# Two transformer blocks in one kernel: products of the weight tiles in chunks of six between the attention steps

## The reference

```python
h = rmsnorm(x, norm_mix[i])
mkv = mem_n @ w_mem_kv[i]                    # 256 memory tokens, 4 heads of 64
proj = h @ w_in[i]                           # q, k, v, qm
y_tok = windowed_gqa(q, k, v, sink)          # i = 0: 12 heads, 4 of k and v, ALiBi, a sink logit
y_tok = neighbourhood_attn(q, k, v, rpb)     # i = 1: 12 heads, a table of biases and a window
y_mem = memory_attn(qm, mk, mv)              # 4 heads
x = x + concatenate([y_tok, y_mem]) @ w_out[i]
gu = rmsnorm(x, norm_ffn[i]) @ w_gate_up[i]
x = x + (silu(gu[:DFF]) * gu[DFF:]) @ w_down[i]
```

## Time and profile before

| | us |
|---|---|
| median of 3 runs | 1098.73 |
| lowest, highest | 1098.53, 1102.89 |
| the profiled execution | 1095.95 |
| its span, first to last instruction | 1094.2 |
| mean granted clock of TensorE | 0.988 |
| busy: PE, VectorE, ScalarE, POOL | 1035.4, 738.4, 585.7, 117.0 |

### The profile page before, as it was taken

The page is one execution under the profiler, slowest core; times in us unless marked ns, Lnnn a source line. Parts: engine busy times, 40 slices in busy tenths (PEclk is TensorE's granted clock), DMA queues, the critical chain, the costliest instruction groups (busy, mean ns, idle before and its releaser), DMA issues.

```text
span 1094.2 us, 13575 instructions
## 1 busy us (share of the span) xinstructions
PE 1035.4 (95%) x5224; PEld 857.8 (78%) x5224; DVE 738.4 (67%) x985; ACT 585.7 (54%) x834; POOL 117.0 (11%) x161
## 2 busy tenths in 40 slices
PE   6997899999999989899999999997989999999996
PEld 5876778789888777788888777886777788888885
DVE  4667774666446577578888766679776766777753
ACT  5557663444345567544443454576656466666641
POOL 1013121000000022200000011013540000000001
PEclk9998999999999999999999989999999999999998
DMA  9655369755565431389989786535365526564541
GB/s 335 202 155 86 106 199 263 244 176 180 166 210 187 152 124 44 114 304 351 353 324 327 288 303 212 164 120 173 125 226 188 183 91 206 178 198 164 171 138 38
DMA packets 98112, 212.42 MB, mean 194 GB/s; under 512 B 5681, under 2 KB 13313, under 8 KB 94657
## 3 DMA queue, kind: packets, MB, share of 16 engines
q1 hardware_dynamic: 93313, 194.46, 52.7%
q0 software_dynamic: 4576, 17.03, 6.4%
q10 hardware_dynamic: 160, 0.07, 0.0%
HBM read 206.82 MB, written 6.15 MB: 195 GB/s over the span
## 4 chain that ended last, share of the span: by engine, by line
PE 67%; DVE 12%; ACT 8%; DMA 5%; issue 5%; POOL 1%; SPq 1%; DVEq 0%; ACTq 0%; POOLq 0%
PE bank L867 20%; PE bank L869 20%; PE bank L868 20%; ACT hi L1191 4%; DVE lo L1619 4%; PE bank L845 3%; DMA raw<-in_w_gate_up 3%; PE bank L881 1%; PE bank L847 1%; DMA raw<-in_w_down 1%; DVE early L1450 1%; DMA raw<-in_w_in 1%; DVE xres L1493 1%; DMA small<-in_sink_a 1%; DVE big L1631 1%
## 5 line engine op out<-in xcount | busy, mean ns | idle before, releaser
L1619 DVE TENSOR_TENSOR lo<-raw,hi 128x2048 fp32r<-128x2048 f32 (+1 forms) x164 | 367.1, 2242 | 220.1 <-ACT hi L1191 219.1
L1191 ACT ACTIVATE hi<-raw 128x2048 fp32r<-128x2048 f32 (+1 forms) x164 | 303.3, 1853 | 191.9 <-PE bank L869 138.5
L867 PE MATMUL bank<-hi,xTh 128*128 128x512 f32 (+2 forms) x896 | 344.9, 385 | 3.5 <-DVE lo L1619 3.4
L869 PE MATMUL bank<-hi,xTl 128*128 128x512 f32 (+2 forms) x896 | 336.3, 375 | 0.0
L868 PE MATMUL bank<-lo,xTh 128*128 128x512 f32 (+2 forms) x896 | 336.1, 375 | 0.0
L867 PEld LDWEIGHTS bank<-hi,xTh 128*128 128x128 f32 x896 | 169.4, 189 | 35.1 <-DVE lo L1619 4.3
L869 PEld LDWEIGHTS bank<-hi,xTl 128*128 128x128 f32 x896 | 169.1, 189 | 31.4
L868 PEld LDWEIGHTS bank<-lo,xTh 128*128 128x128 f32 x896 | 169.5, 189 | 28.2
L867 PE MATMUL bank<-hi,hTh 128*128 128x512 f32 x264 | 103.5, 392 | 0.7 <-DVE lo L1619 0.7
L869 PE MATMUL bank<-hi,hTl 128*128 128x512 f32 x264 | 102.8, 389 | 0.0
L868 PE MATMUL bank<-lo,hTh 128*128 128x512 f32 x264 | 102.8, 389 | 0.0
(11 more groups left out here) (353 smaller groups left out, 1352.8 us busy)
## 6 DMA issues: line engine op xcount, KB each, us to landing
raw<-in_w_gate_up SPq DMA_DIRECT2D x44, 1024.0 KB, 5.7
raw<-in_w_down SPq DMA_DIRECT2D x30, 1024.0 KB, 5.1
raw<-in_w_ada SPq DMA_DIRECT2D x24, 1024.0 KB, 6.6
raw<-in_w_up SPq DMA_DIRECT2D x22, 1024.0 KB, 5.2
raw<-in_w_in SPq DMA_DIRECT2D x21, 1024.0 KB, 5.0
raw<-in_w_out SPq DMA_DIRECT2D x12, 1024.0 KB, 5.1
raw<-in_w_in_b SPq DMA_DIRECT2D x10, 1024.0 KB, 5.1
raw<-in_w_in_a SPq DMA_DIRECT2D x6, 1024.0 KB, 9.9
```

The lines of the kernel that those rows point to most:

```text
L867: e.matmul(o, sh, h[:, k, :], start=p.first and k == 0, stop=False)
L869: done = e.matmul(o, sl, h[:, k, :], start=False, stop=p.last and k == p.nk - 1)
L1191: e.activation(hi_s[m % SPLITS][:, 0:n], raw[p.at % RAWS][:, 0:n], ACT.Copy).then_inc(hi_made, 1)
L1619: e.tensor_tensor(lo_s[s][:, 0:n], raw[p.at % RAWS][:, 0:n], hi_s[s][:, 0:n].bitcast(F), ALU.subtract).then_inc(lo_made, 1)
```

## The change

The table of tiles now has the size of a chunk in blocks, and for each gap letters: `p` takes the next thing from the queue, `a` the next attention step, from a queue of its own (`heads`). After the first tile or two, all parts of both mixes (and of the memory tile between them) come in chunks of two blocks, six products, with a step or a pair in most gaps; so have the four parts of each output projection, with a step in every gap and behind every part. The demand for channels 4 to 7 before the output projection is gone: each block asks for its own channel. Three of the four output parts go through their blocks by channel, both halves of the tokens in turn (first the memory heads' channels 6 and 7); the fourth still does one half of the tokens and then the other. In the second layer the v tile (1536) comes last of the five. The work is the same.

```diff
-MIX_TILES = [[(1024, 4, 2), (512, 4, 1), (0, 0, 1)], [(2048, 4, 2), (1536, 0, 1), (512, 0, 1), (1024, 4, 1), (0, 0, 1)]]
+MIX_TILES = [[(1024, 4, ["pp", "pp", "pp"]), (512, 4, ["p", "pa", "a"]), (0, 2, ["p", "a", "p", "a", "p", "a", "a"])],
+             [(2048, 4, ["pp", "pp", "pp"]), (512, 4, ["p", "pa", "a"]), (1024, 2, ["p", "a", "p", "a", "", "", ""]),
+              (0, 2, ["p", "p", "a", "a", "a", "a", ""]), (1536, 2, ["p", "p", "a", "a", "a", "a", "a"])]]
+MEMORY_1 = ["p", "a", "p", "a", "a", "a", "a"]
...
+        self.chunks = (2 * nk + size - 1) // size
+        if tile.kind == "out" and (k0 or tile.c == 0):
+            ks = (2, 3, 0, 1) if k0 else (0, 1, 2, 3)
+            self.blocks = [(t, k) for k in ks for t in range(2)]
+        else:
+            self.blocks = [(t, k) for t in range(2) for k in range(nk)]
...
     def need(self, tag):
         while tag not in self.made:
-            self.put(*self.later.popleft())
+            if tag[0][0] == "y" and self.heads:
+                self.head()
+            else:
+                self.put(*self.later.popleft())
...
         for k in range(2):
             for n in range(2):
                 if k == 0:
-                    for at in range(4, 8):
-                        self.need((("y", l), at))
                     made.append(self.tile("out", l, 512 * n, 512))
-                self.part(made[n], ("y", l), k == 0, k == 1, self.pop)
+                self.part(made[n], ("y", l), k == 0, k == 1, self.head, 2)
                 if k == 1:
                     self.evacuate(made[n])
-                self.pop(3)
+                self.head()
         self.drain()
+
+    def head(self):
+
+        if self.heads:
+            self.put(*self.heads.popleft())
+        else:
+            self.pop()
```

More of the change, by code:

```diff
@@ L148, in __init__ @@
         self.res_at = {}
+        self.heads = deque()
         self.run()
@@ L348, in tile, with part @@
         return t
-    def part(self, tile, source, first, last, between):
+    def part(self, tile, source, first, last, between, size=4):
         m = len(self.parts)
@@ L353, in part @@
         _, k0, nk, w = self.plan[i][1]
-        p = Part(m, i, tile, source, first, last, k0, nk, w)
+        p = Part(m, i, tile, source, first, last, k0, nk, w, size)
         self.parts.append(p)
         for ch in range(p.chunks):
-            for n in range(4 * ch, min(4 * ch + 4, 2 * nk)):
-                self.need((source, k0 + n % nk))
+            for _, k in p.chunk(ch):
+                self.need((source, k0 + k))
             self.steps.append(("mm", m, ch))
@@ L396, in evacuate, with linear @@
             self.later.extend(("cv", c, l, k) for k in range(0, t.w // 128, 2))
-    def linear(self, kind, l, c, w, parts, source, pops=1, hooks=None):
+    def linear(self, kind, l, c, w, parts, source, pops=1, hooks=None, size=4, heads=None):
         t = self.tile(kind, l, c, w)
-        hooks = deque(hooks or [])
+        hooks, letters = deque(hooks or []), deque(heads or [])
         def between():
-            if hooks:
+            if letters:
+                for x in letters.popleft():
+                    self.pop() if x == "p" else self.head()
+            elif hooks:
                 for name in hooks.popleft().split():
@@ L410, in linear @@
             self.hold = p == parts - 1 and c == 512 and kind in ("lastdown", "out2")
-            self.part(t, source, p == 0, p == parts - 1, between)
+            self.part(t, source, p == 0, p == parts - 1, between, size)
             if p == parts - 1:
@@ L436, in mix @@
         kinds = {0: {1024: "vm", 512: "k", 0: "q"}, 1: {2048: "vm", 1536: "v", 512: "q", 1024: "q", 0: "q"}}[l]
[L437 to L442, removed]
+        self.heads = deque(("att", l, i) for i in range(23))
+        for n, (c, size, heads) in enumerate(MIX_TILES[l]):
+            self.linear(kinds[c], l, c, 512, 2, ("in", 2 * l), size=size, heads=heads)
+            if n == 0:
                 self.later.append(("blank",))
-            for _ in range(heads):
-                self.later.append(steps.popleft())
-        self.later.extend(steps)
         if l == 0:
             self.put("rel")
-            self.linear("mem", 1, 0, 512, 2, "mem", 1)
+            self.linear("mem", 1, 0, 512, 2, "mem", size=2, heads=MEMORY_1)
         made = []
@@ L862, in matmuls @@
                         e.wait_ge(*ready(p.source, p.k0 + k))
-                    if p.first and k == 0:
+                    if p.first and opens:
                         await_bank(e, ("tile", t_.j, t))
```

19 lines of the change are left out of this document (10 added, 9 removed).

## The result

The changed kernel takes 1104.63 us (median of 20 runs, 1100.99 to 1110.38), the kernel before 1098.57 us beside it (20 runs). The ratio is 1.0065, with a 95% interval of 1.005 to 1.008. By the ratio the change makes the kernel slower by 0.65%, some 7 us (the two medians lie 6.1 us apart); the forecast was 1098.6 us, no difference. The profiled execution has a span of 1100.1 us.

The account below looks back on a forecast made before the run. PE was taken as the chain for 67% of the span, its attention waits set by the VectorE-ScalarE softmax loop. First layer -1.55 and second layer with hand-over +1.6 sum to nothing: 1098.6 us, range 1086 to 1107.

Parts of the forecast that it names:

- The price of a split in the loop: VectorE's first-layer attention steps with a weight split between them are 6.67 us apart in place of 2.66, costing 4.0 us.
- rival A: ScalarE's split copy falls into its idle time and doesn't lengthen the loop; 12.1 us won, 1086.5 us; chance 0.30.
- Step 4: First layer: PE's scores wait 3.5 us for keys until 70.0; the clock then falls for some 3.4 us, costing 1.7.
- Steps 9 and 12: First layer: PE's transposes wait 2.35 and 2.75 us because VectorE has a split between the steps before.
- waits for banks of head outputs: First layer, steps 10 and 12: banks of head outputs that VectorE has just to read, 0.85 us each.
- the last channel: First layer's first output projection part: its last channel waits 1.2 us for heads 6 and 7, made by step 13.
- Five small ones from step 16 on: First layer: five small PE waits at the end of the list, 1.75 us in all.
- First layer: 0.15 - 1.7: First layer: waits of 14.15 us against 14.3 today win 0.15; one clock fall costs 1.7; slower by 1.55 us.
- rival C: Leftover waits at steps 4 and 12 and the second layer's step 14 lower the clock; 8.5 us, 1107 us; chance 0.17.
- step 14 of the second layer: PE waits 2.3 us for the reciprocal behind a split, and 0.8 us for a bank.
- Second layer and hand-over: Second layer's waits 6.7 us against 7.1, won 0.4; hand-over to the ffn wins 1.2; sum 1.6 us.
- Blocks by channels: Output projections of both layers: alternating PE between two banks costs 0, with bounds of 0 to 5.8 us.

Follow-up runs that it names:

- the two runs at clock 1.00: Zero products in four first-layer waits of the change (1101.19 us); 128-column products ahead of steps 5, 6 and 8 in the kernel before (1097.97 us).
- three lows late: The change with VectorE's half of first-layer splits 13, 14 and 15 alone one gap later; 1098.76 us, ratio 1.0009 to the kernel before.
- two lows late: The change with VectorE's half of first-layer splits 10 and 11 alone one gap later; 1103.3 us, ratio 1.006 to the kernel before.
- products in the four waits: The change with products of zeros ahead of the first layer's step 4 scores and steps 9, 12 and 15; 1101.19 us, ratio 1.0036.
- second output tile later: The change with the first layer's second output tile opened, and its first chunk multiplied, two steps later; 1103.31 us, ratio 1.0053.
- late half: The change with VectorE's half of each split in both layers one gap later, behind the next step; 1095.59 us, ratio 0.9988.
- mixed order: First layer ordered as before, second as changed, VectorE's split halves one gap later, products ahead of first-layer steps 5 and 6; 1092.67 us, ratio 0.9963.
- the pair earlier: The change with VectorE's split halves one gap later, plus the first layer's third pair of keys made ahead of step 3; 1095.3 us, ratio 0.997.

## Why the prediction was wrong

**The price of a split in the loop: right.** Two steps with a split between them are 6.65 us apart on VectorE (88.55 to 95.20), forecast 6.67. ScalarE's copy is in the loop, so rival A was wrong.

**Step 4: the wait right, the fall twice as long.** PE waited 3.92 us for kTl, its scores began at 70.04 (forecast 3.5 and 70.0). "So the wait of 3.5 us at step 4 makes it fall, at 1.2 in place of 2.4 GHz for 3.4 us or so": it was 6.83 us.

**Steps 9 and 12: right in size.** 2.58 and 2.74 us, forecast 2.35 and 2.75. Their times were not: PE was there at 94.67 and 109.34 us (forecast 91.6 and 104.8). PE and VectorE had come late by the same amount, and in the difference this drops out. The waits for banks of head outputs (0.85 each at steps 10 and 12) and for the last channel (1.2) did not come; step 11 waited 0.47 for a bank, step 6 0.5 for 0.9.

**Step 15: missed.** The list of waits ended with "Five small ones from step 16 on". A split lies between steps 14 and 15 as between 8 and 9 and between 11 and 12. I had let PE come late enough to step 15 to find it ready; it waited 3.14 us. Opening the tile later moved that wait to step 16 (3.26 us), so it belongs to the split, not to the bank.

**The clock: the step that failed.** It is the line "First layer: 0.15 - 1.7", and both of its terms. The 1.7 counts one fall of 3.4 us, but in the profiled execution the waits of 2.6 to 3.1 us at steps 9, 12 and 15 each had one too. I had read from the earlier trace rows that after an idle time of 2.45 us the clock stayed at 1.00. That was one execution: the same wait was 2.43 and 2.44 us in two other kernels with that order of the second layer, and the clock fell there (460.39 and 453.07). So the row could not carry the forecast of one fall. The further falls I gave to rival C. Its place at step 4 and step 12 was right; its third, step 14 of the second layer, did not fall behind 1.97 us in the change, but did in three other executions of that order. The error in the other term, 0.15: the 14.3 us of "today" included 3.4 us of half clock as something to be won. The kernel before with products in its waits has no fall and takes the same 103.92 us. That loss was no loss, because the loop on VectorE set the pace there.

Put together: the 0.15 was -3.3 without those 3.4 us; step 15 makes it worse by 3.1, the terms that did not come better by some 2, which gives the 4.3 us that the two runs at clock 1.00 measure; and the clock costs 5.1 in place of 1.7. Sum 9.4 against 1.55. Of the 7.85 us between, 3.4 are clock (of the 5.1 that rival C adds in this layer), and some 4.4 are waits, which no rival had. That C's 1107 us comes near the measured time is in part luck.

**Second layer and hand-over: nearly right.** PE's wait for the last additions fell from 2.45 to 1.11 us (forecast 0.8), and the layer won 1.1 us of 1.6:

```profile
461.08 0.55 PE L864 MATMUL bank<-const,xres 128*128 128x128 f32 x3 [1.11 <-DVE xres L1512]
```

Step 14 waited 1.97 us, forecast 2.3. The gain hangs on the clock. Counted from its first tile, the layer takes 120.80 us before and 119.70, 119.69 and 119.70 in the three executions of the new order (the change, three lows late, two lows late) without a fall; in three others (first layer as before, products in the four waits, second output tile later) the clock fell at step 14 and it takes 120.97, 120.79 and 120.88. Step 14's wait is the same in both, here the change and the kernel with the first layer as before:

```profile
428.34 0.52 PE L864 MATMUL bank<-const,gbc 128*128 128x128 f32 x3 [1.97 <-DVE pl L1410]
428.76:432.17 3.41, 3.16 (x26) 2.62 (x25) 2.77 (x13) 2.54 (x8) 1.84 (x4) 1.00 0.74 280
...
421.10 0.52 PE L890 MATMUL bank<-const,gbc 128*128 128x128 f32 x3 [1.98 <-DVE pl L1436]
421.52:424.93 3.41, 3.23 (x21) 2.76 (x20) 2.59 (x12) 1.53 (x5) 1.85 (x4) 0.50 0.75 284
```

One fall of 3.41 us thus costs 1.1 to 1.3 us there, as much as the new order wins. With the late half in both layers the second takes 118.70 us in place of 119.70, counted from its first tile, so the splits cost it about one microsecond, too.

**Blocks by channels: right at 0.** At full clock the six products of a chunk of the output parts take 1.14 to 1.24 us from the start of the first to the start of the last, those of other tiles 1.16 to 1.28, so the change of bank costs nothing where up to 5.8 us stood in the bounds. The pattern that the Trainium skill describes under "A second HAM failure mode: psum-queue depth-cycling" (TensorE: Matmul & The Clock Gate), a clock that oscillates on cycling banks, didn't show: every fall in the layer begins in a wait for VectorE or behind one.

Of the signs named in advance, the wait at step 4, the 6.7 us between steps and the second layer came; the first gate tile did not (155.07 us, forecast 146 to 149). The range, 1086 to 1107, holds the median of 1104.6. What was wrong is its middle, and the chance of 0.20 for "slower".

## What to carry to other kernels

Products between the steps of a pipeline fill PE's small waits, but whatever else is emitted with them (here a weight split with a wait inside) lands in the loop of the engines that set the pace. Give each engine its own place for its half of such a pair: put the producer's half where it is and the consumer's half one gap later, so that the consumer never stands still in a queue that others wait on. In the kernel before, where steps 4 to 13 have no split between them, this was worth nothing that could be told. And before the time at a half clock is counted as something to win, ask who sets the pace there: 6.83 us of it cost nothing where VectorE did. Whether a wait brings a fall isn't read from one trace.

## What was not expected of the hardware

In the change's profiled execution the clock fell at each of the first layer's idle times of 2.6 to 3.1 us, for 3.41 us, and at 3.92 us for 6.83; with products of 0.86 us each in them it stayed at 1.00. In the kernel before, two waits of 0.97 and 1.77 us close together (92.28 and 94.68; 1.31 us busy of 3.41) had the effect of one long one: the clock fell in the second, for 6.83 us. In the mixed order, with 0.88 and 1.83 us there, it stayed at 1.00.

The same wait doesn't do it every time. Over all profiled executions, in the two layers: at PE's waits of 2.7 us and more the clock fell each time (16 of 16), at those of 2.4 to 2.6 us in 4 of 8, at those of 1.7 to 2.1 us in 9 of 26. A fall is counted when it begins in the wait or within 2.1 us behind it. Step 9's 2.6 us, step 14's 1.98 us in the second layer and the last additions' 2.4 us each came out both ways with the same order of work.

Where the clock falls isn't the same in every execution. Behind the two layers, where all kernels but two have the same work, the profiled executions have between 3 and 6 falls ahead of the last one: the kernel before at 647.00, 749.40 and 889.35 us, the one with its order in the first layer at 650.21, 749.20, 766.27, 800.40 and 889.15. Twelve executions of one kernel (the pair earlier) lie between mean clocks of 0.980 and 0.991 and between 1089.55 and 1097.95 us. The scatter of the runs of one kernel, some 0.8%, is of this size, which is why differences under 0.2% stay open here.
